# Hybrid pool/SSD decoder layer: the causal mask of the decay matrices moved from two TensorE matmuls per step to a clamp on ScalarE and a triangle product on VectorE

## What is computed

```python
# CHUNK = 128, 4 groups (g), 6 heads per group (r), head width 64, state 128
a_cs  = jnp.cumsum(d * a, axis=2)                  # a < 0, d > 0: falls along the chunk
causal = jnp.tril(jnp.ones((CHUNK, CHUNK), dtype=bool))
seg   = a_cs[:, :, :, None] - a_cs[:, :, None, :]
decay = jnp.exp(jnp.where(causal[None, None, :, :, None, None], seg, -jnp.inf))
cb    = jnp.einsum('bclgn,bcsgn->bclsg', cc, bc)
y_diag = jnp.einsum('bclsgr,bcsgrp->bclgrp', cb[..., None] * decay, xdt)
...
y_off  = jnp.einsum('bclgn,bcgrpn,bclgr->bclgrp', cc, prev, jnp.exp(a_cs))
```

## Time and profile before

| what | value |
|---|---|
| median of 3 runs | 2904.22 us (2899.64 to 2907.06) |
| the profiled execution | 2906.24 us |
| its span in the trace | 2904.4 us |
| mean granted clock of TensorE over the span | 0.986 of full |
| TensorE busy | 97% of the span |
| VectorE, GpSimd, ScalarE busy | 58%, 51%, 45% |
| matmuls L1675, all 128 | 50.7 us busy, overlapping their neighbours |

### The profile page before, as it was taken

The page is one execution under the profiler, slowest core; times in us unless marked ns, Lnnn a source line. Parts: engine busy times, 40 slices in busy tenths (PEclk is TensorE's granted clock), DMA queues, the critical chain, the costliest instruction groups (busy, mean ns, idle before and its releaser), DMA issues.

```text
span 2904.4 us, 35702 instructions
## 1 busy us (share of the span) xinstructions
PE 2813.1 (97%) x13310; PEld 2309.0 (79%) x13310; DVE 1698.4 (58%) x2173; ACT 1310.0 (45%) x2244; POOL 1482.6 (51%) x955
## 2 busy tenths in 40 slices
PE   8999999999999999999999999999999799999998
PEld 6688877888778887878877778877888688888887
DVE  4577723777427775157773546655444466667667
ACT  2355534555446554365552544454445322222223
POOL 1365543555445554446555657766555435343433
PEclk9999999999999999999999999999999899999999
DMA  8322133422234222342213346555444742333323
GB/s 239 102 73 66 53 115 109 131 70 62 95 109 138 67 72 80 99 156 73 66 59 131 123 167 218 188 186 177 144 153 170 301 159 102 145 116 131 109 102 145
DMA packets 289290, 363.03 MB, mean 125 GB/s; under 512 B 8906, under 2 KB 214350, under 8 KB 280030
## 3 DMA queue, kind: packets, MB, share of 16 engines
q1 hardware_dynamic: 289118, 360.75, 37.4%
HBM read 272.64 MB, written 88.08 MB: 124 GB/s over the span
## 4 chain that ended last, share of the span: by engine, by line
PE 90%; POOL 2%; DVE 2%; issue 1%; DMA 1%; ACT 1%; DVEq 0%; SPq 0%; ACTq 0%; POOLq 0%
PE bank L1616 26%; PE bank L1899 20%; PE bank L1867 20%; PE bank L1641 11%; PE bank L1723 2%; PE bank L1728 2%; PE bank L1707 1%; PE bank L1691 1%; PE bank L1737 1%; PE bank L1675 1%; PE bank L1699 1%; PE bank L1680 1%; POOL w_lo L434 1%; PE bank L1713 1%; DMA third<-T_scr 1%
## 5 line engine op out<-in xcount | busy, mean ns | idle before, releaser
L434 POOL TENSOR_TENSOR w_lo<-raw,w_hi 128x1024 fp32r<-128x1024 f32 x208 | 506.8, 2437 | 657.2 <-ACT w_hi L426 657.2
L426 ACT ACTIVATE w_hi<-raw 128x1024 fp32r<-128x1024 f32 x208 | 220.0, 1058 | 575.5 <-PE bank L1616 333.8
L1616 PE MATMUL bank<-hnT_hi,w_hi 128*128 128x512 f32 x1152 | 462.6, 402 | 3.5 <-ACT pre L1260 3.5
L1616 PE MATMUL bank<-hnT_hi,w_lo 128*128 128x512 f32 x1152 | 450.3, 391 | 0.0
L1616 PE MATMUL bank<-hnT_lo,w_hi 128*128 128x512 f32 x1152 | 449.7, 390 | 0.0
L1921 DVE SCALAR_TENSOR_TENSOR acc<-pre,par,acc 128x512 f32<-128x512 f32 x240 | 251.6, 1048 | 120.9 <-ACT pre L1260 114.8
L1899 PE MATMUL bank<-w_first,T_hi 128*128 128x512 f32 x896 | 275.9, 389 | 0.4 <-DVE T_lo L2205 0.4
L1616 PEld LDWEIGHTS bank<-hnT_hi,w_hi 128*128 128x128 f32 x1152 | 217.1, 188 | 46.5 <-issue 4.4
L1616 PEld LDWEIGHTS bank<-hnT_hi,w_lo 128*128 128x128 f32 x1152 | 216.5, 188 | 46.7
L1616 PEld LDWEIGHTS bank<-hnT_lo,w_hi 128*128 128x128 f32 x1152 | 217.2, 189 | 41.9
L2223 DVE TENSOR_TENSOR acc_th<-bank,acc_th 128x512 f32<-128x512 f32 x224 | 150.2, 686 | 160.6 <-PE bank L1899 160.4
(11 more groups left out here) (296 smaller groups left out, 6248.0 us busy)
## 6 DMA issues: line engine op xcount, KB each, us to landing
raw<-in_w_in SPq DMA_DIRECT2D x168, 512.0 KB, 3.9
T_scr<-stage SPq DMA_DIRECT2D x32, 1792.0 KB, 6.7
pair_raw<-in_w_ff SPq DMA_DIRECT2D x36, 1024.0 KB, 5.4
raw<-in_w_out SPq DMA_DIRECT2D x64, 512.0 KB, 3.5
third<-T_scr SPq DMA_DIRECT2D x28, 1024.0 KB, 4.8
pair_raw<-T_scr SPq DMA_DIRECT2D x28, 1024.0 KB, 4.8
w_raw<-in_w_ff SPq DMA_DIRECT2D x12, 1024.0 KB, 8.4
h<-in_x SPq DMA_DIRECT2D x5, 2048.0 KB, 10.8
```

What stands on the lines that cost most here:

```text
L426: nc.scalar.activation(w_hi[:, N % 2, :], raw[:, N % RING, :], ACT.Copy).then_inc(w_hi_ready, 1)
L434: nc.gpsimd.tensor_tensor(w_lo[:, N % 2, :], raw[:, N % RING, :], w_hi[:, N % 2, :].bitcast(F32), ALU.subtract).then_inc(w_lo_ready, 1)
L1616: mm = nc.tensor.matmul(bank[s][:, :], w[:, k, :], t[:, k, :], start=(k == 0 and j == 0), stop=(k == KT - 1 and j == 2))
```

## The change

The two matmuls L1675 go, and with them `ident_r`, `barred`, `below` and FAR. The matmuls L1680 now start their banks. ScalarE reads the banks with Relu of -seg into E, signals `fall_ready`, waits for it itself and takes Exp of -E in place, so that the exponent is clamped at zero. TensorE's next `slot1` and the first output unit wait for `fall_ready` where they waited for `exp_ready`. VectorE multiplies the C.B product by `tri` in bank 3, waits for that, then waits for `exp_ready` and multiplies E as before.

```diff
-FAR = -1e30
...
-        ident_r = sb("ident_r", [P, P], F32R)
-        barred = sb("barred", [P, P], F32R)
...
+        fall_ready = sig("fall_ready", STEPS)
...
-                pool.affine_select(out=below[:, :], in_=ones[:, :], compare_op=ALU.is_gt,
-                                   fill=0.0, base=0, pattern=[[-1, P]], channel_multiplier=1)
...
-                nc.vector.tensor_copy(ident_r[:, :], ident[:, :])
-                nc.vector.tensor_scalar(barred[:, :], below, FAR, None, ALU.mult)
...
                         nc.scalar.activation(
                             E[:, :, :].rearrange("p (j r) l -> p j (r l)", j=2),
-                            decay_ps[:, :, 0:GW], ACT.Exp).then_inc(exp_ready.sem, 1)
+                            decay_ps[:, :, 0:GW], ACT.Relu, scale=-1.0).then_inc(fall_ready.sem, 1)
+                        fall_ready.wait(act, b, q + 1)
+                        nc.scalar.activation(
+                            E[:, :, :], E[:, :, :], ACT.Exp, scale=-1.0).then_inc(exp_ready.sem, 1)
...
-                    exp_ready.wait(pe, b, q)
-                    for j in range(2):
-                        nc.tensor.matmul(
-                            bank[4 + j][:, 0:GW].rearrange("p (r l) -> p r l", l=P),
-                            ident_r[:, :], barred[:, :].unsqueeze(1).to_broadcast([P, 3, P]),
-                            start=True, stop=False)
+                    fall_ready.wait(pe, b, q)
                     for j in range(2):
                         mm = nc.tensor.matmul(
                             bank[4 + j][:, 0:GW].rearrange("p (r l) -> p r l", l=P),
                             seg_s[:, g % 2, cols], seg_l[:, c, 3 * j:3 * j + 3, :],
-                            start=False, stop=True)
+                            start=True, stop=True)
...
-                            exp_ready.wait(pe, b, STEPS)
+                            fall_ready.wait(pe, b, STEPS)
...
                         zs_ready.wait(dve, b, q + 1)
+                        cb = bank[3][:, GW:GW + P]
+                        steps.link(nc.vector.tensor_tensor(cb, cb, tri[:, :], ALU.mult))
+
+
+                        exp_ready.wait(dve, b, q + 1)
                         nc.vector.tensor_tensor(
-                            E[:, :, :], E[:, :, :],
-                            bank[3][:, GW:GW + P].unsqueeze(1).to_broadcast(
+                            E[:, :, :], E[:, :, :], cb.unsqueeze(1).to_broadcast(
                                 [P, HEADS_PER_GROUP, P]), ALU.mult).then_inc(g_ready.sem, 1)
```

More of the change, by code:

```diff
@@ L365, in build @@
         wdt = F[:, 6084:6276].rearrange("p (k c) -> p k c", c=HEADS)
-        below = F[:, 5956:6084]
         prow = F[:, 5700:5956].rearrange("p (s c) -> p s c", c=P)
```

## The result

The changed kernel takes 2914.7 us, the median of 12 runs (2912.4 to 2917.6), where 12 runs of the kernel before have 2906.5 (2899.6 to 2909.7). The ratio is 1.0032, with a 95% interval of 1.0023 to 1.0041: a little slower. I had forecast 2886.5 and a range that ended at 2894.

What follows compares the result with a forecast made beforehand. TensorE, busy 2813 of 2904 us, was taken as the bound. The terms -17.3 - 0.6 + 0 = -17.9 us took the profiled 2906.2 to 2888.3 and the median to 2886.3, stated as 2886.5 us; range 2878 to 2894.

Steps and rivals of the forecast that it cites:

- The pair's worth: Removing the two L1675 matmuls saves TensorE 0.36 us a step, paid in full in 48 steps (0 to 11): 17.3 us.
- Steps 12 to 15: Step 12 gains nothing; steps 13 to 15 gain 0.05 us each, 0.6 in all, the other 0.31 becoming L1691 waits.
- ScalarE: Relu plus Exp adds 0.94 us a step (0.73 to 1.2), covered by idle 1.29 us, or 1.20 in steps 13 to 15.
- VectorE, steps 0 to 11: The 128x128 triangle multiply adds 0.34 us (0.2 to 0.5) a step, covered because yo and the taps stand waiting.
- The second rival: VectorE and GpSimd disturbance uses up steps 0 to 11's cover: 8.6 us lost (2895), at worst 2904; chance 0.14.
- The tail: Step 15, VectorE's chain to yo: the multiply costs 0, at most 1.4 us, with 0.59 us of room before L434.
- The clock rival: New waits in steps 12 to 15 halve TensorE's clock, 2.2 us a fall, 16 falls giving 2922; chance 0.04.

Runs made afterwards that it cites:

- the changed kernel with the copies in the wrong place: Changed kernel plus two unread 128-column ScalarE copies in step 1 of each block, ahead of the first w_hi, where ScalarE stands idle: 2913.0 us, ratio 1.0031.

## Why the forecast failed

- **The pair's worth**, 0.36 us a step by starts: right, and what the fp32 product in front adds did pass to the next pair (L1671 now takes the 0.65 us). Steps 1 and 4 to 11 shorten by 0.34 to 0.37; the pair's removal alone gives 20 us (forecast 17.9, within the interval).
- **Steps 12 to 15**, 0.00 and 0.05 us: right, and the new waits are the ones named (0.63 us in step 12, 0.30 in step 13).
- **ScalarE**: right. The split makes xb 0.92 us later behind the bank's first reader (forecast 0.94; 1.61 in place of 0.69 us in the kernel with the split alone), and that kernel is unchanged. The new Exp takes 0.847 us (taken as 0.845).
- **VectorE, steps 0 to 11**: this step failed. I wrote that "yo and the taps stand waiting for TensorE and ScalarE", and read it from steps in the middle of a block. In step 0 VectorE works off the seg_l products, and from there to the yo of step 1 it does not pause once. I had costed the product's 0.3 us as hidden without looking at the step with the least room.
- **The second rival** had the mechanism, VectorE and GpSimd holding each other up, and the wrong price. I let a lost cover cost at most the 0.36 us that it would have hidden, 2904 at worst. A lost race costs what is left of the other engine's instruction, here 2.0 to 2.2 us each time a w_lo was ahead, whatever the size of the delay that lost it, and step 1 loses two of them. Four waits of 3.4 us and the clock behind them gave 23.7 us back.
- **That the saving itself was the second ingredient** was in no rival. TensorE's saving brings w_hi and w_lo of step 1 forward by 0.4 us against a VectorE chain that does not move with them. Priced part by part, the change is a gain; no sum of parts can show a race between two of them.
- **The tail**, 0 to 1.4 us: the room was named, but only the product's own 0.3 was set against it, and not the delay that comes from step 14. The wait for yo grew by 2.9 us.
- **The clock rival** was right that a wait can take more than its length, and put it in steps 12 to 15, where waits of 0.3 to 0.7 us left the clock whole (1.00 in every stretch from 322 to 358).

What stays open: the 3.8 us behind the last step of block 3. Of them 0.85 is the longer wait for yo (3.31 against 2.46 us) and 1.6 a longer wait for w_lo in the output projection (2.10 against 0.52 us). That wait is hardly the change's: the total of such waits is 3.9 us here and 2.3 in the kernel before, but 4.0 in the kernel with the split alone and in the kernel before with the seg_l row moved, and 2.3 in the changed kernel with the copies in the wrong place. No run looked for its cause. The rest was not taken apart, nor were the 1.9 us (29.4 - 23.7 - 3.8) that lie mostly between the blocks and ahead of the first.

## What to carry to other kernels

Where two engines exclude each other, an edit's cost isn't its length: look for pairs of starts on the two engines that lie within the edit's delay or saving of each other, in the fullest step and not in a typical one, and price a swapped pair at up to the length of the instruction that gets ahead, and once more for the next pair that this delay swaps. Speeding up the bottleneck moves such pairs as well as adding work does. If a change gives back what it saved at one place per loop, look there for work without a near deadline (here a seg_l row and two F columns), and check whose deadline is next behind the one that you relieve.

## What the runs showed of the hardware

Added work made a kernel faster: 0.49 us more on ScalarE, four times, took some 20 us off it, by moving one GpSimd start in each block from 0.26 us ahead of a VectorE start to 0.15 behind it. The outcome is decided at hundredths of a us: 0.04 us ahead was enough for F to pass untouched (0.69 us), and 0.03 behind held it for 2.87. And a stop of 3.4 us in the middle of dense work was followed by 4 us at half of TensorE's clock in block 0, and in all four blocks by a fall of some length, so that it cost 5.4 to 6.6 us (steps 2 and 3 are 35.9 to 37.2 us together, where two undisturbed ones are 30.5) and not 3.4.
